# Sixteen experts in a row on TensorE, third weights behind the first gathers, and routing in two parts

## The reference, cut to what matters

```python
scores = jax.nn.sigmoid((xt @ w_router).astype(jnp.float32))
sel = (scores + b_router.astype(jnp.float32)).reshape(n_tok, N_GROUPS, EXPERTS_PER_GROUP)
group_score = lax.top_k(sel, 2)[0].sum(-1)
grp = jnp.argmax(group_score, axis=-1).astype(jnp.int32)
...
_, local = lax.top_k(in_grp, TOP_K)
expert_idx = grp[:, None] * EXPERTS_PER_GROUP + local.astype(jnp.int32)
gate = jnp.take_along_axis(scores, expert_idx, axis=1)
gate = gate / gate.sum(-1, keepdims=True)
...
def expert_block(args):
    xblk, e = args
    hg, hu = jnp.split(xblk @ w_exp_in[e], 2, axis=-1)
    return (jax.nn.silu(hg) * hu) @ w_exp_out[e]
...
return jnp.einsum('tk,tkd->td', gate.astype(x.dtype), y_assign).reshape(shape)
```

## Time and profile before

| | |
|---|---|
| median of 3 runs | 2396.8 us (2393.5 to 2406.75) |
| the profiled execution's own time | 2399.68 us |
| its span | 2397.8 us |
| PE, DVE, ACT, POOL busy | 89%, 41%, 18%, 11% of the span |
| mean rate of DMA | 160 GB/s |

### The profile page before, as it was taken

How to read it: one execution, slowest core, us unless ns; L and a number is a source line. 1 busy time by engine, 2 the same in 40 slices (tenths; PEclk the granted TensorE clock), 3 DMA queues, 4 the chain that set the end, 5 groups by cost and what they waited for, 6 DMA issues and landing times. The chain is left out here.

```text
span 2397.8 us, 52103 instructions
## 1 busy us (share of the span) xinstructions
PE 2143.7 (89%) x21084; PEld 1363.4 (57%) x21085; DVE 974.0 (41%) x1930; ACT 429.0 (18%) x890; POOL 261.9 (11%) x430
## 2 busy tenths in 40 slices
PE   5999999939999998999988998899898499899987
PEld 3666654426666665466555555666444366576653
DVE  1333233352222221649866668345333422222226
ACT  1223221100000001211114554333211000000011
POOL 0000000002122221102010000000000122122212
PEclk9999999969999999999999999899999699999999
DMA  6111214167768763721030001654332558755847
GB/s 217 37 36 36 87 65 156 53 225 269 287 262 332 287 229 107 280 75 39 18 114 7 7 5 45 232 197 158 119 119 88 197 198 321 293 213 187 345 155 289
DMA packets 148590, 382.89 MB, mean 160 GB/s; under 512 B 11592, under 2 KB 71128, under 8 KB 146472
## 3 DMA queue, kind: packets, MB, share of 16 engines
q1 hardware_dynamic: 110160, 276.62, 31.0%
q0 software_dynamic: 16480, 82.77, 9.3%
q10 hardware_dynamic: 21880, 22.55, 2.8%
HBM read 336.89 MB, written 45.00 MB: 159 GB/s over the span
## 5 line engine op out<-in xcount | busy, mean ns | idle before, releaser
L306 PE MATMUL PS<-xT,W 128*128 128x352 f32 x960 | 287.1, 462 | 29.1 <-ACTq L315 29.1
L501 PE MATMUL PS<-wo,yT 128*128 128x512 f32 x576 | 261.2, 603 | 0.6 <-issue 0.6
L306 PEld LDWEIGHTS PS<-xT,W 128*128 128x128 f32 x960 | 183.4, 191 | 131.1 <-ACTq L315 28.7
L790 PE MATMUL PS<-xT,yst 128*32 128x256 f32 x3648 | 211.7, 383 | 28.2 <-DVE yst L861 17.9
L801 PE MATMUL PS<-w,yst 128*32 128x256 f32 x3360 | 203.6, 379 | 15.3 <-DVE yst L876 14.9
L861 DVE STREAM_TRANSPOSE yst<-yst 128x256 f32<-128x256 f32 x150 | 66.8, 445 | 352.6 <-PE PS L790 335.3
L1031 PE MATMUL PS<-xT,W 128*128 128x352 f32 (+1 forms) x672 | 202.6, 464 | 1.2 <-ACT xT L976 1.2
L790 PEld LDWEIGHTS PS<-xT,yst 128*32 128x32 f32 x3648 | 141.8, 111 | 88.6 <-issue 37.9
L790 PE MATMUL PS<-yT,yst 128*32 128x256 f32 x3072 | 176.3, 379 | 11.8 <-issue 11.8
L836 ACT ACTIVATE yst<-PS 128x128 f32<-128x128 f32 x150 | 41.6, 277 | 804.8 <-PE PS L790 683.9
L501 PEld LDWEIGHTS PS<-wo,yT 128*128 128x128 f32 x576 | 106.5, 192 | 119.1 <-issue 119.0
(11 more groups left out here) (365 smaller groups left out, 2470.1 us busy)
## 6 DMA issues: line engine op xcount, KB each, us to landing
xT<-in_w_exp_in SPq DMA_DIRECT2D x24, 2048.0 KB, 14.6
w<-in_w_exp_out SPq DMA_DIRECT2D x22, 2048.0 KB, 14.1
yT<-in_w_exp_in SPq DMA_DIRECT2D x20, 2048.0 KB, 12.8
wo<-in_w_exp_in SPq DMA_DIRECT2D x20, 2048.0 KB
xrn<-in_w_exp_out SPq DMA_DIRECT2D x10, 2048.0 KB, 14.7
yb<-yst ACTq DMA_DIRECT2D x150, 128.0 KB
W<-in_w_in_even SPq DMA_DIRECT2D x20, 512.0 KB, 4.0
xm<-xrn SPq DMA_DIRECT2D x18, 512.0 KB, 2.9
```

The costliest lines, as they stand in the source:

```text
L306: ins = nc.tensor.matmul(PS[:, n % 5, 0:CW], W5[:, p, k, :], xT[:, k, c * CW:(c + 1) * CW], start=(k == 0), stop=(k == KD - 1))
L501: ins = nc.tensor.matmul(PS[:, mix_bank(t) + n, :], yT[:, (k + 4 * l) % KD, t * P:(t + 1) * P], wo[:, k, n * 512:(n + 1) * 512], start=(fi ...
L790: ins = nc.tensor.matmul(PS[q * GR:(q + 1) * GR, 0, 0:2 * P], xtb[:, k, :], w1[s][:, k, q * 2 * P:(q + 1) * 2 * P], start=(k == 0), stop=( ...
```

## The change

PE's experts stand in a row of 16 in its program, with an inner loop over the granules of each, and PE reads one number per expert, the first granule of the next, behind the first `up` of the present one; the count is the difference of two such numbers. SP waits for the second transposed granule (`xtb`) before it loads the third weights. In the routing ACT takes the sigmoid of eight tiles ahead of the ninth's transpose, DVE chooses for eight tiles and then for the ninth, a scan over the tiles takes the place of the nine sums, PE adds the counts of the earlier tiles by a further matmul, the weighted one-hot array is the one of 32 rows, the table is summed in four column groups of 32 and folded by one more matmul, and the gates are computed after the table.

```diff
+                if t == NT - 1:
+                    act.wait_ge(sem("m_lg"), 1 + 9 * l + t)
+                    nc.scalar.activation(rt[0][:, 0:t, :], logits[:, 0:t, :], ACT.Sigmoid).then_inc(sem("r_sig"), 1)
...
+            D(TS(by_expert(pos), cst[:, C_LANE:C_LANE + NT].unsqueeze(2).broadcast_to([P, NT, EXPERTS]), 1.0, None, ALU.min))
+            dve.wait_ge(sem("r_sig"), 2 * l + 1)
+            D(select(0, NT - 1))
+            dve.wait_ge(sem("r_sig"), 2 * l + 2)
+            D(select(NT - 1, NT))
...
+            D(nc.vector.tensor_tensor_scan(upto, mask, chosen, 0.0, ALU.mult, ALU.add))
+            TT(before, upto, chosen, ALU.subtract).then_inc(sem("r_chosen"), 1)
             dve.wait_ge(sem("r_count"), l + 1)
-            for t in range(NT):
-                D(TT(cum[:, t + 1, :], cum[:, t, :], PS[:, 1, t * EXPERTS:(t + 1) * EXPERTS], ALU.add))
...
-            D(TT(pos[:, :, :], cum[:, 0:NT, :], PS[:, 0, 0:NT * EXPERTS].rearrange("p (t e) -> p t e", e=EXPERTS), ALU.add))
...
-            D(TT(ohh, cst[:, C_ROW:C_ROW + NB].unsqueeze(1).broadcast_to([P, 2 * NT, NB]), wide(hif[:, :], NB), ALU.is_equal))
-            D(TT(ohh, ohh, wide(cst[:, C_TOK:C_TOK + 2 * NT], NB), ALU.mult))
+            D(TT(ohl, cst[:, C_LANE:C_LANE + GR].unsqueeze(1).broadcast_to([P, 2 * NT, GR]), wide(lof[:, :], GR), ALU.is_equal))
+            D(TT(ohl, ohl, wide(cst[:, C_TOK:C_TOK + 2 * NT], GR), ALU.mult))
             for q in range(0, 2 * NT, 6):
-                TT(ohl[:, q:q + 6, :], cst[:, C_LANE:C_LANE + P].unsqueeze(1).broadcast_to([P, 6, P]), wide(lof[:, q:q + 6], P),
+                TT(ohh[:, q:q + 6, :], cst[:, C_ROW:C_ROW + NB].unsqueeze(1).broadcast_to([P, 6, NB]), wide(hif[:, q:q + 6], NB),
                    ALU.is_equal).then_inc(sem("r_place"), 1)
...
+            nc.tensor.matmul(PS[:, 1, 0:EXPERTS], ones, upto[:, NT - 1, :], start=True, stop=True)
+            nc.tensor.matmul(PS[:, 0, 0:NT * EXPERTS], tri, a, start=True, stop=False)
+            nc.tensor.matmul(PS[:, 0, 0:NT * EXPERTS], ones, before, start=False, stop=True).then_inc(sem("r_count"), 1)
...
-                ins = nc.tensor.matmul(PS[:, 2, 0:NB], ohl[:, q, :], ohh[:, q, :], start=(q == 0), stop=(q == 2 * NT - 1))
+                ins = nc.tensor.matmul(PS[j * GR:(j + 1) * GR, 2, 0:NB], ohl[:, q, :], ohh[:, q, :], start=(q < 4), stop=(q >= 2 * NT - 4))
             ins.then_inc(sem("r_table"), 1)
+            pe.wait_ge(sem("r_lanes"), l + 1)
+            nc.tensor.matmul(PS[:, 3, 0:NB], cst[:, C_FOLD:C_FOLD + P], lanes, start=True, stop=True).then_inc(sem("r_table"), 1)
...
             sp.wait_ge(sem("r_plan"), l + 1)
+            sp.wait_ge(sem(f"e{l}_xtb"), 2 + 2)
             load_w1(sp, l * EXPERTS + 2, 2)
             load_w2(sp, l * EXPERTS + 2, 2)
...
-                n = pe.value_load(plan[0:1, e:e + 1] if isinstance(e, int) else plan[0:1, bass.ds(e, 1)], min_val=2, max_val=MAX_GR)
-                g0 = 0 if begin else first_of(pe, e)
+            g0, following = 0, first_of(pe, 1)
+            for e in range(EXPERTS):
+                s, turn = e % 3, e // 3
                 per = 5 if s else 6
                 pe.wait_ge(sem(f"e_in_w1_{s}"), 32 * per * l + turn * 32 + 32)
                 part(pe)
                 up(s, g0)
-                if not begin:
+                if e > 0:
+                    following = first_of(pe, e + 1) if e + 1 < EXPERTS else total_of(pe)
                     down((s + 2) % 3, g0 - 1)
                 pe.wait_ge(sem(f"e_in_w2_{s}"), 16 * per * l + turn * 16 + 16)
                 part(pe)
+                n = nc.s_assert_within(following - g0, 2, MAX_GR, skip_runtime_bounds_check_because="every expert has two granules or more in the plan")
                 with pe.Fori(0, n - 1) as j:
...
-            with pe.Fori(0, EXPERTS // 3) as i:
-                expert(i * 3 + 1, 1, i, False)
-                expert(i * 3 + 2, 2, i, False)
-                expert(i * 3 + 3, 0, i + 1, False)
-            down(0, total_of(pe) - 1)
+                g0 = following
+            down(0, g0 - 1)
```

More of the change, by code:

```diff
@@ L621, in dve_route @@
             TR = nc.vector.tensor_reduce
[L622 to L657, removed]
+            def by_expert(x):
+                return x[:, :, :].rearrange("p t e -> p (t e)").rearrange("p (e t) -> p t e", t=NT)
@@ new lines, in select, with first_max @@
+            def select(t0, t1):
+                n_t, ts = t1 - t0, slice(t0, t1)
+                D(TT(sel[:, ts, :], sc[:, ts, :], brt[:, :].unsqueeze(1).broadcast_to([P, n_t, EXPERTS]), ALU.add))
+                q = sel[:, ts, :].rearrange("p t (g e) -> p (t g) e", e=PER_GROUP)
+                r = [x[:, ts, :].rearrange("p t g -> p (t g)") for x in rs]
+                D(TT(r[0], q[:, :, 0], q[:, :, 1], ALU.max))
+                D(TT(r[1], q[:, :, 0], q[:, :, 1], ALU.min))
+                D(TT(r[2], q[:, :, 2], q[:, :, 3], ALU.max))
+                D(TT(r[3], q[:, :, 2], q[:, :, 3], ALU.min))
+                D(TT(r[4], r[0], r[2], ALU.max))
+                D(TT(r[0], r[0], r[2], ALU.min))
+                D(TT(r[1], r[1], r[3], ALU.max))
+                D(TT(r[0], r[0], r[1], ALU.max))
+                D(TT(r[4], r[4], r[0], ALU.add))
+                def first_max(dst, x, iota, n, work):
+                    D(TR(rk[0][:, ts, :], x, AX.X, ALU.max))
+                    D(TT(dst, x, rk[0][:, ts, 0:1].broadcast_to([P, n_t, n]), ALU.is_equal))
+                    D(TT(work, dst, iota.unsqueeze(1).broadcast_to([P, n_t, n]), ALU.mult))
+                    D(TR(rk[1][:, ts, :], work, AX.X, ALU.max))
+                    D(TT(dst, work, rk[1][:, ts, 0:1].broadcast_to([P, n_t, n]), ALU.is_equal))
+                i4, i16 = cst[:, C_IOTA4:C_IOTA4 + 4], cst[:, C_IOTA:C_IOTA + 16]
+                first_max(rs[1][:, ts, :], rs[4][:, ts, :], i4, 4, rs[2][:, ts, :])
+                D(TS(rs[3][:, ts, :], rs[1][:, ts, :], 1.0, BIG, ALU.subtract, ALU.mult))
+                mq = m[:, ts, :].rearrange("p t (g e) -> p (t g) e", e=PER_GROUP)
+                D(TT(mq, q, wide(r[1], PER_GROUP), ALU.mult))
+                D(TT(mq, mq, wide(r[3], PER_GROUP), ALU.add))
+                first_max(oh1[:, ts, :], m[:, ts, :], i16, 16, eq[:, ts, :])
+                D(mul_add(m[:, ts, :], oh1[:, ts, :], -3.0 * BIG, m[:, ts, :]))
+                first_max(oh2[:, ts, :], m[:, ts, :], i16, 16, eq[:, ts, :])
+                D(TT(A[:, ts, :], oh1[:, ts, :], oh2[:, ts, :], ALU.add))
+                return TT(by_expert(tmp)[:, ts, :], A[:, ts, :], wide(cst[:, C_VALID + t0:C_VALID + t1], EXPERTS), ALU.mult)
@@ new lines, in dve_route @@
+            D(TS(by_expert(pos), cst[:, C_LANE:C_LANE + NT].unsqueeze(2).broadcast_to([P, NT, EXPERTS]), 1.0, None, ALU.min))
[3 more added lines that the diff above has]
+            D(select(NT - 1, NT))
+            upto = cum[:, 0:NT, :].rearrange("p t e -> p (t e)")
+            chosen, before, mask = (x[:, :, :].rearrange("p t e -> p (t e)") for x in (tmp, eq, pos))
+            D(nc.vector.tensor_tensor_scan(upto, mask, chosen, 0.0, ALU.mult, ALU.add))
@@ L696, in dve_route @@
             D(nc.vector.tensor_copy(plan[:, 32:48], cnt[2][:, :]))
+            dve.wait_ge(sem("r_table"), 2 * l + 2)
+            TS(table[:, :], PS[:, 3, 0:NB], float(QU), cst[:, C_QUART:C_QUART + 1], ALU.mult, ALU.add).then_inc(sem("r_plan"), 1)
             for k, oh in enumerate((oh1, oh2)):
@@ L803, in down @@
                 ins.then_inc(sem(u + "down"), 1)
-            def expert(e, s, turn, begin):
-                n = pe.value_load(plan[0:1, e:e + 1] if isinstance(e, int) else plan[0:1, bass.ds(e, 1)], min_val=2, max_val=MAX_GR)
-                g0 = 0 if begin else first_of(pe, e)
+            g0, following = 0, first_of(pe, 1)
+            for e in range(EXPERTS):
+                s, turn = e % 3, e // 3
                 per = 5 if s else 6
@@ L820, in expert @@
                     down(s, g)
-            expert(0, 0, 0, True)
-            with pe.Fori(0, EXPERTS // 3) as i:
-                expert(i * 3 + 1, 1, i, False)
-                expert(i * 3 + 2, 2, i, False)
-                expert(i * 3 + 3, 0, i + 1, False)
-            down(0, total_of(pe) - 1)
+                g0 = following
+            down(0, g0 - 1)
         def act_experts(act, l):
```

19 lines of the change are left out of this document (10 added, 9 removed).

## The result

The changed kernel took 2376.1 us in the median of seven executions (2368.0 to 2383.0), beside 2396.8 before: a ratio of 0.990, with an interval of 0.988 to 0.992. It is faster by some 21 us by the medians and 24 by the ratio, inside the range and 6 us above the predicted 2370. The profiled execution after is the shortest of the seven (2368.0, span 2366.1 against 2397.8). The readings that follow are therefore taken from stretches, not from the spans.

A forecast was written before the change was run, and what follows sets the result against it. PE was taken as busy nearly throughout, with waits in routing and at expert boundaries, where stores often set the pace. Gains 23.0 - 0.3 + 6 = 28.7 us gave 2371 from the profile, 2368 from the median; forecast 2370, range 2350 to 2382.

The forecast's parts named there:

- The start of the layers: From last layer norm to first `up`: 8.6 plus 2.9 us shorter per layer, 23.0 for both.
- the choice with scan and subtraction: Routing on DVE: choice in two parts ends at 1870.7, 0.3 us gained (bounds -2.6 and +2.7).
- The counts: Routing: one more matmul, the nine sums and one operation of 144 elements go; 1.95 us gained net.
- One-hots and table: Routing: smaller operations and four overlapping column groups take 5.7 us in place of 12.0; 6.3 gained.
- the routing: Choice, counts, one-hots and table together: 8.6 us gained per layer (bounds 11 and 1).
- The third weights: SP's 6 MB load moved behind the first gathers: L861 starts 2.9 us earlier per layer (0 to 3.9).
- The collision: Delayed third weights meeting stores and next weights: priced at 0.3 us for both layers; as rival 5 less, 2375, chance 0.05.
- The boundaries: Between experts: PE's 27.9 us idle goes, mostly returning as waits for L876; 6.4 gained, 6 after bare reads.
- the prediction's own example: First layer's first boundary: room of 0.33 us before `down`, so 0.33 of a nearly 1 us gap comes off.
- slow gathers: Start of layers: first gathers stay slow for a reason other than weights; 5.8 us less, 2376, chance 0.05.
- a read that is not early: Behind each first `up`: the read is uncovered, 0.7 us each eats the boundaries' 6; 2376, chance 0.03.
- Instruction fetch: PE's sixteen straight expert bodies: 24 packets per layer, at 2.7 us wait each 97 us slower, 2467; chance 0.03.

The follow-up runs named there:

- one-part kernel: Changed kernel with the choice of experts made at once for all nine tiles, after the second sigmoid: 2375.9 us, ratio 0.9907.
- the row alone: Kernel before with only TensorE's expert program changed (sixteen experts in a row, one plan number read behind each first `up`): 2402.6 us, ratio 1.0021.
- the row and four buffers: Kernel before with TensorE's experts in a row and four staging buffers for stores, granule loops in groups of four: 2368.1 us, ratio 0.9879.
- the third weights early: Changed kernel without SP's wait for the second transposed granule before it loads the third expert's weights: 2383.3 us, ratio 0.9940.
- two reads: Changed kernel with two plan numbers read ahead of each expert's `up` after the first expert: 2382.7 us, ratio 0.9925.
- the loop with early reads: Kernel before with its expert loop kept, ten of the fifteen boundaries' reads moved behind `up`: 2404.8 us, ratio 1.0026.
- the routing alone: Kernel before with only the routing rewritten, expert loop and place of the third weights kept: 2385.5 us, ratio 0.9943.

## Why the prediction was right, and where it was not

**The start of the layers: right.** By its own steps, from the end of the layer norm: the choice with scan and subtraction was to end 16.1 later (1870.7 against 1854.63) and ended 16.1 later (1852.37 against 1836.27); first part 8.98 with its mask (9.0 foreseen), second 6.25 (6.2), scan 0.46 (0.5). The counts gave 1.8 (8.81 before from the end of the choice to the first one-hot, 7.01 after) for 1.95. One-hots and table took 5.93 for 5.7, and the four column groups do overlap: L739 ends 0.94 behind DVE's last operand. L713 starts 29.04 behind the layer norm, where 29 was said, and `up` 5.79 behind L713, where 5.7 was said. The starts gave 10.9 and 11.0, 21.9 together for 23.0 (taken apart, the routing 7.4 and 7.9 where 8.6 was said, and the third weights more than was said: the two misses cancel in part); that the first part of the choice earns only what the second costs was foreseen too, and the one-part kernel shows it.

**The third weights: right, a little too low.** 2.9 per layer foreseen, 3.7 and 3.5 to 3.6 by the kernel without the wait. The collision that the prediction priced at 0.3 is below what two profiles of one kernel differ by, and so is not shown.

**The boundaries: the mechanism right, the term of the sum wrong.** The prediction said that most of the idle time would return as waits for L876 because the stores set the pace, and that these would rise from 19 to some 40. They rose to 43.7. But it read the room at each of the 30 boundaries and let 6.4 us of it come off; the row alone lost 5, and the changed kernel's two profiles have experts 1.2 and 6.2 us longer than before. This term, 6 less foreseen and 1 to 6 more measured, is what the sum misses most by (28.7 foreseen, 21 to 24 measured). The step that failed is that a landing two granules on "is not moved by what PE does in the gap", so that the room left before the next `down` could be had at least. What the runs show in its place: the delays ahead of `down` grew by 35 us (22.5 to 57.5 and 57.6) for the 34.3 taken off the boundaries, so none of the room was had. At the prediction's own example the landing did move, in the one execution that was profiled of each kernel. SP asks for the weights at 557.64 before and at 558.38 with the row alone:

```profile
557.64 0.93 SPq L740 DMA_DIRECT2D xT<-in_w_exp_in  x2
```

```profile
558.38 0.93 SPq L740 DMA_DIRECT2D xT<-in_w_exp_in  x2
...
579.57 0.42 DVE L872 COPY yst<-PS 128x256 f32<-128x256 f32 x1 [3.54 <-DMA yb<-yst]
...
580.14 1.93 PE L801 MATMUL PS<-w,yst 128*32 128x256 f32 x32 [1.10 <-DVE yst L872]
```

The copy that ends the wait begins 20.74 behind that before and 21.19 with the row: 0.45 later, more than the 0.33 of room. Over both layers the sum is 56.7 to 64.7 in all ten profiles with two buffers, however little of it stands at the boundaries (0 to 34.3); with the row and four buffers 0.2 of it is left, beside 13 us of waits for the gated product and for weights in the second layer. That is the shape of it: with two buffers the stores set at least this sum, and idle time counts as part of it. On one point the prediction is nearer to the trace than the kernel's description ahead of it: the weights of expert e are asked for at the last `up` of expert e-3, just before the boundary (L740 at 1931.14, the next `up` at 1933.77), and not behind the first `up` of expert e-2.

**What is luck.** Three of the prediction's small rivals (slow gathers, a read that is not early, a collision) put the time at 2375 or 2376, and 2376 was measured. The rows show none of the three: the gathers landed mostly in 2.8 us, the waits behind the first `up` are the stores', and the experts are no quicker with the third weights early. The time alone would not have told them from what happened.

**Instruction fetch: rightly left out.** The packets rose to 25, as foreseen (24). With four buffers the same 16 bodies kept PE busy in 396.6 of 398.3 us, and with two the account of the experts closes without them. The Trainium skill (Runtime: NRT & Kernel Launch, Instruction fetch mechanics) says that crossing a block of 16 KiB is mostly hidden; this trace agrees, at 0.41 MB in 25 packets.

**What stays open.** Why the sum goes up to 61.5 and 64.7 in one part and two reads and stays at 57 to 60 in the rest; where bursts of weights begin against the stores may do it, but nothing here sets that apart. Why the clock fell behind some long waits for a copy and not behind others: one part has three of 2.2 to 2.7 us in the first layer's experts and no fall behind them. And the medians of the row alone and of the loop with early reads lie 5 to 6 us above before, where the experts of their one profile account for 2.9.

## What to carry to other kernels

Idle time of the bounding engine is worth taking away only where nothing else would make it wait at that place: add the engine's idle time and its waits for the next resource over the stretch, and ask whether the sum or only its division will change. Here the same edit lost 5 us with two staging buffers and gained 26 with four, so the buffer comes first and the boundaries second. A chain in which every step waits for the one before, as at the start of each layer, is the other case: there each microsecond taken off a step, or off a transfer that delays it, came off the total, within the spread (with the routing alone 15.3 us off the starts and some 14 off the time).

## What the runs showed of the hardware

A store of 128 KB in a burst of weights landed after 11.9 to 13.5 us with two in flight and after 23.6 and 26.0 with four, one per 6 to 7 us in both: queueing more hid the latency and did not shorten it. In such a burst with four in flight, the issue of a store held ACT's queue for 2.0 to 3.05 us, where it mostly takes 0.56, and PE then went on at 6.3 to 6.8 us per granule in place of 5.2. Behind waits for a copy of 2.1 and 2.7 us the granted clock fell from 1.00 to 0.50 for 3.4 us, which cost PE half of that. Two executions of one kernel differed by 6.5 us (902.6 and 909.1) in the 900 us from the end of the first layer's experts to the last layer norm of the second, at mean granted clocks of 0.963 and 0.958 over the span; this spread, not the few rows around the change, is what bounds a comparison of two profiles.
